# Nine pairs behind six plain units in the first projection, and a new order around its last pair

## The reference, cut to what matters

```python
def short_conv_fourier_mixer(h, w_in, conv_w, w_out):
    proj = h @ w_in                                  # 1024 -> 3072
    a_x, a_b, a_c, a_z, b_u, b_z = jnp.split(proj, ...)   # six parts of 512
    y_a = a_b * centred_depthwise_conv(a_c * a_x, conv_w) * jax.nn.silu(a_z)
    u = b_u.reshape(bsz, s, B_GROUPS, B_GROUP_DIM)
    f = jnp.fft.fft2(u, axes=(1, 3), norm="ortho").real
    y_b = f.reshape(bsz, s, B_WIDTH) * jax.nn.silu(b_z)
    return jnp.concatenate([y_a, y_b], axis=-1) @ w_out
x = x + short_conv_fourier_mixer(rms_norm(x, norm_even[i]), ...)
```

## Time and profile before

| What | us |
|---|---|
| median of three runs | 1758.22 |
| the profiled execution | 1759.79 |
| its span, first to last instruction | 1757.9 |
| PE busy | 1693.6 (96%) |
| VectorE (DVE) busy | 1158.4 (66%) |
| ScalarE (ACT) busy | 684.8 (39%) |
| GpSimd (POOL) busy | 486.8 (28%) |
| mean granted TensorE clock | 0.987 |
| PE's share of the chain that ended last | 83% |
| a load of w_raw, issue to landing | 4.1 |

### The profile page before, as it was taken

How to read it: one execution, slowest core, us unless ns; L and a number is a source line. 1 busy time by engine, 2 the same in 40 slices (tenths; PEclk the granted TensorE clock), 3 DMA queues, 4 the chain that set the end, 5 groups by cost and what they waited for, 6 DMA issues and landing times.

```text
span 1757.9 us, 21497 instructions
## 1 busy us (share of the span) xinstructions
PE 1693.6 (96%) x8228; PEld 1399.7 (80%) x8228; DVE 1158.4 (66%) x1421; ACT 684.8 (39%) x878; POOL 486.8 (28%) x348
## 2 busy tenths in 40 slices
PE   7699999899999999999899999999999999999997
PEld 6488887788788888888788877788888788878885
DVE  7867887445677777777876698345645267788323
ACT  7121112225566555666632422101123667772002
POOL 4244554233201111101013323223324322214330
PEclk9799999899999999999999999999999999999998
DMA  5011116132101111011242211112123311336102
GB/s 224 1 72 49 72 72 226 50 120 85 48 1 37 36 37 34 3 37 37 104 167 96 84 48 40 45 66 72 68 80 131 125 49 61 120 131 240 48 25 96
DMA packets 41829, 137.92 MB, mean 78 GB/s; under 512 B 5644, under 2 KB 6028, under 8 KB 41472
## 3 DMA queue, kind: packets, MB, share of 16 engines
q1 hardware_dynamic: 41440, 136.02, 21.5%
q10 hardware_dynamic: 288, 0.52, 0.1%
HBM read 104.81 MB, written 31.59 MB: 78 GB/s over the span
## 4 chain that ended last, share of the span: by engine, by line
PE 83%; DVE 11%; ACT 3%; issue 2%; DMA 0%; DVEq 0%; SPq 0%; ACTq 0%
PE pair L977 34%; PE pair L1164 11%; PE pair L1239 8%; PE pair L1302 5%; PE aux L1275 4%; PE pair L1288 3%; PE pair L988 2%; PE pair L1583 2%; PE aux L1454 1%; PE pair L996 1%; PE pair L1052 1%; PE aux L977 1%; PE pair L1568 1%; DVE stat_b L2558 1%; PE pair L1596 1%
## 5 line engine op out<-in xcount | busy, mean ns | idle before, releaser
L842 POOL CAST w_hi<-w_raw 128x1024 fp32r<-128x1024 f32 x86 | 96.4, 1121 | 942.0 <-issue 937.0
L844 POOL TENSOR_TENSOR w_lo<-w_raw,w_hi 128x1024 fp32r<-128x1024 f32 x86 | 217.3, 2527 | 6.9
L977 PE MATMUL pair<-op_hi,w_hi 128*128 128x512 f32 x670 | 207.4, 391 | 1.0 <-DVE op_lo L2202 0.7
L977 PE MATMUL pair<-op_lo,w_hi 128*128 128x512 f32 x670 | 206.9, 390 | 0.0
L977 PE MATMUL pair<-op_hi,w_lo 128*128 128x512 f32 x670 | 206.8, 390 | 0.0
L977 PEld LDWEIGHTS pair<-op_hi,w_hi 128*128 128x128 f32 x670 | 125.7, 188 | 30.0 <-issue 3.0
L977 PEld LDWEIGHTS pair<-op_hi,w_lo 128*128 128x128 f32 x670 | 126.0, 188 | 26.5
L977 PEld LDWEIGHTS pair<-op_lo,w_hi 128*128 128x128 f32 x670 | 126.1, 188 | 26.4
L1897 ACT ACTIVATE pt_hi<-pair 128x1024 fp32r<-128x1024 f32 x60 | 61.6, 1027 | 126.9 <-issue 84.7
L2197 DVE TENSOR_TENSOR pt_lo<-pair,pt_hi 128x1024 fp32r<-128x1024 f32 x60 | 73.5, 1224 | 52.7 <-ACT pt_hi L1897 48.9
L1239 PE MATMUL pair<-opb_hi,w_hi 128*128 128x512 f32 x256 | 101.8, 397 | 1.1 <-DVEq L136 0.6
(11 more groups left out here) (463 smaller groups left out, 3806.8 us busy)
## 6 DMA issues: line engine op xcount, KB each, us to landing
w_raw<-weight_units SPq DMA_DIRECT2D x106, 512.0 KB, 4.1
xa<-x_t SPq DMA_DIRECT2D x15, 512.0 KB, 7.7
xf<-y_dram SPq DMA_DIRECT2D x12, 512.0 KB, 4.6
x_dram<-xa SPq DMA_DIRECT2D x8, 512.0 KB, 5.8
xc<-x_dram SPq DMA_DIRECT2D x8, 512.0 KB, 7.8
x_dram<-xc SPq DMA_DIRECT2D x8, 512.0 KB, 2.7
y_dram<-y_d SPq DMA_DIRECT2D x8, 512.0 KB, 2.7
mz_dram<-y_d SPq DMA_DIRECT2D x8, 512.0 KB, 2.9
```

Of the source, the lines that this page charges most:

```text
L842: pool.tensor_copy(w_hi[:, u % 2, :], w_raw[:, u % RAW, :]).then_inc(w_hi_done, 1)
L844: pool.tensor_tensor(w_lo[:, u % 2, :], w_raw[:, u % RAW, :], w_hi[:, u % 2, :], ALU.subtract).then_inc(w_split, 1)
L977: mm = pe.matmul(acc[:, cols], w, x[:, kx, cols], start=(first and k == 0 and n == 0), stop=(last and k == KT - 1 and n == 2))
```

## The change

FAST becomes 6, so units 0 to 5 are plain and make the whole of group 0, and nine pairs follow. mixer_of, copy_at, the skipped slot in ring and GpSimd's wait behind it are renumbered to that. PE makes both transforms of group 0 among the plain units: over channels behind unit 4, over time behind unit 5. VectorE's queue ahead of the pairs holds folding, convolution, scalings and both outputs of group 0, with the operand sums and the first weight sums between them. In the last pair ScalarE makes high parts 0 and 1 of the second projection's operand between the copies of P5 and P6; VectorE makes the last group's fourier_output and low parts 0 and 1 between add_c11 and add_c22, and low parts 2 and 3 between add_c22 and add_c12.

```diff
--- before.py
+++ after.py
@@ -56,7 +56,7 @@
 UNITS = BASE[-1]
 
 
-FAST = 4
+FAST = 6
 PAIRS = (EVEN_IN - FAST) // 2
 QUAD = KT // 2
 RING_STEP = 8
@@ -90,13 +90,13 @@
 
 def copy_at(q, name):
 
-    order = ("P1", "P6", "P5") if q % 3 == 1 else ("P1", "P5", "P6")
+    order = ("P1", "P6", "P5") if q % 3 == 0 else ("P1", "P5", "P6")
     return COPIES + 3 * q + order.index(name) + 1
 
 
 def ring(at):
 
-    return (at + (2 if at >= RING_STEP else 0)) % 4
+    return (at + (1 if at >= RING_STEP else 0)) % 4
 
 
 def plain(n):
@@ -533,7 +533,7 @@
 
         def mixer_of(q):
 
-            return (q + 2) // 3, (q + 2) % 3
+            return q // 3 + 1, q % 3
 
         def updates(d):
 
@@ -889,7 +889,7 @@
                 if at < 4:
                     pool.wait_ge(unit_done, FAST - 1 + half)
                 else:
-                    pool.wait_ge(product_done, at - 1 if at - RING_STEP in (0, 1) else at - 3)
+                    pool.wait_ge(product_done, at - 2 if at - RING_STEP in (0, 1, 2) else at - 3)
                 pool.tensor_copy(hi, src).then_inc(w_hi_done, 1)
                 if name not in SUM_OF:
                     pool.wait_ge(w_hi_done, FAST + at + 1)
@@ -1168,15 +1168,16 @@
 
             for u in range(2, FAST):
                 unit(u, u, op_hi, op_lo, "even")
+                if u == FAST - 2:
+                    fft_channels(0)
+            fft_time(0)
             for q in range(PAIRS):
                 j, turn_of = mixer_of(q)
                 product(q, "P1")
                 if q >= 1:
                     product(q - 1, "P4")
                 product(q, "P5")
-                if q == 1:
-                    fft_time(0)
-                elif q >= 3 and turn_of == 2:
+                if turn_of == 2:
                     fft_time(j)
                 product(q, "P6")
                 product(q, "P2")
@@ -1184,8 +1185,6 @@
                     fft_channels(j)
                 product(q, "P7")
                 product(q, "P3")
-                if q == 0:
-                    fft_channels(0)
             product(PAIRS - 1, "P4")
             first_pair(BASE[1], "y1", op_hi, op_lo)
             for e in range(2, KT):
@@ -1738,7 +1737,7 @@
                 if kind == 0:
                     act.wait_ge(parts_ready, j)
                 elif kind == 1:
-                    act.wait_ge(c22_added, q - 1)
+                    act.wait_ge(c22_added, max(q - 1, 1))
                 else:
                     act.wait_ge(parts_ready, j + 1)
                 product_copy(q, "P1", first_row[kind][:, 0:HALF])
@@ -1779,26 +1778,28 @@
                 act.wait_ge(scaled_a, j + 1)
                 link(act.activation(y_a[:, 1, :], y_a[:, 1, :], ACT.Silu), silu_a)
 
-            copy_p1(0)
-            copy_p5(0)
-            copy_u2(0)
+            spectrum(0)
             fourier_gate(0)
-            spectrum(0)
-            for q in range(1, PAIRS):
+            conv_gate(0)
+            for q in range(PAIRS):
                 j, kind = mixer_of(q)
                 copy_p1(q)
                 if kind == 0:
-                    conv_gate(j - 1)
+                    if j >= 2:
+                        conv_gate(j - 1)
                     copy_u2(q)
                     copy_p5(q)
                     continue
                 if kind == 2:
                     fourier_gate(j)
                 copy_p5(q)
+                if q == PAIRS - 1:
+                    for k in range(2):
+                        y_hi("y1", k, y1_in[k], op_hi)
                 copy_u2(q)
                 if kind == 1:
                     spectrum(j)
-            for k in range(THROUGH["y1"]):
+            for k in range(2, THROUGH["y1"]):
                 y_hi("y1", k, y1_in[k], op_hi)
             conv_gate(AB - 1)
             for k in range(THROUGH["y1"], KT):
@@ -2383,29 +2384,38 @@
 
             dve.wait_ge(ax_ready, 1)
             by_token(ax_sb[:, :], ax_sb[:, :])
-            for n in range(3):
-                weight_sum(0, n)
             wait_job(dve, 2)
             link(dve.tensor_tensor(u_pad[:, 1:S + 1], pair[0][:, :], ax_sb[:, :], ALU.mult))
             free(2)
+            dve.wait_ge(bu_ready, 1)
+            fold_parts(0)
+            convolve(0)
             dve.wait_ge(copied, QUAD + 3)
             link(dve.tensor_tensor(xa_cmb[:, 0:QUAD, right], xa[:, 0:QUAD, right], xa_cmb[:, 0:QUAD, left], ALU.subtract),
                  cmb_low)
+            wait_job(dve, 4)
+            link(dve.tensor_tensor(cv[:, :], pair[0][:, :], cv[:, :], ALU.mult))
+            free(4)
+            for n in range(3):
+                weight_sum(0, n)
+            dve.wait_ge(ax_ready, 2)
+            by_token(sz_b[:, :], sz_b[:, :])
+            signal(scaled_b)
             dve.wait_ge(copied, QUAD + 2)
             link(dve.tensor_tensor(cmb_lo[:, 1], cmb_raw[:, 1], cmb_hi[:, 1], ALU.subtract), cmb_low)
             sum_low_part(0, "P5")
+            wait_job(dve, 5)
+            by_token(y_a[:, 1, :], pair[1][:, :])
+            signal(scaled_a)
+            free(5)
             sum_low_part(0, "P6")
             weight_sum(0, 3)
-            convolve(0)
+            fourier_output(0)
+            conv_output(0)
+            sum_low_part(0, "P7")
             dve.wait_ge(copied, QUAD + 4)
             link(dve.tensor_tensor(xa_cmb[:, QUAD:KT, left], xa[:, QUAD:KT, left], xa_cmb[:, QUAD:KT, right], ALU.subtract),
                  cmb_low)
-            sum_low_part(0, "P7")
-            dve.wait_ge(bu_ready, 1)
-            fold_parts(0)
-            dve.wait_ge(ax_ready, 2)
-            by_token(sz_b[:, :], sz_b[:, :])
-            signal(scaled_b)
             for q in range(PAIRS):
                 j, kind = mixer_of(q)
                 sum_low_part(q, "P3")
@@ -2413,9 +2423,16 @@
                 if q + 1 < PAIRS:
                     weight_sum(q + 1, 0)
                     weight_sum(q + 1, 1)
+                else:
+                    fourier_output(j)
+                    for k in range(2):
+                        low(k, y1_in[k], OP0["y1"])
                 add_c22(q)
                 if q + 1 < PAIRS:
                     sum_low_part(q + 1, "P5")
+                else:
+                    for k in range(2, QUAD):
+                        low(k, y1_in[k], OP0["y1"])
                 add_c12(q)
                 if q + 1 < PAIRS:
                     sum_low_part(q + 1, "P6")
@@ -2424,26 +2441,19 @@
                 if kind == 0:
                     fold_parts(j)
                     take_c21(q)
-                    if q + 1 < PAIRS:
-                        sum_low_part(q + 1, "P7")
+                    sum_low_part(q + 1, "P7")
                 elif kind == 1:
                     link(dve.tensor_tensor(u_pad[:, 1:S + 1], u_pad[:, 1:S + 1], ax_sb[:, :], ALU.mult))
                     convolve(j)
                     take_c21(q)
-                    if q + 1 < PAIRS:
-                        sum_low_part(q + 1, "P7")
+                    sum_low_part(q + 1, "P7")
                     signal(scaled_b)
                 else:
                     link(dve.tensor_tensor(cv[:, :], ab_row, cv[:, :], ALU.mult))
-                    if j == AB - 1:
-                        fourier_output(j)
-                        for k in range(QUAD):
-                            low(k, y1_in[k], OP0["y1"])
                     take_c21(q)
-                    if q + 1 < PAIRS:
-                        sum_low_part(q + 1, "P7")
                     signal(scaled_a)
                     if j < AB - 1:
+                        sum_low_part(q + 1, "P7")
                         fourier_output(j)
                     else:
                         for k in range(QUAD, THROUGH["y1"]):
```

## The result

The changed kernel takes 1741.75 us (median of four, 1741.51 to 1743.92) where the kernel before takes 1758.83 beside it: the ratio is 0.9905, 95% interval 0.9887 to 0.9922, so 17.1 us less. I forecast 1734 with a range of 1729 to 1741. The direction was right, and the gain is 70% of the 24.6 us forecast; the time lies 0.75 us above the range.

The account below looks back on a forecast made before the run. PE's time line bounds the kernel, its losses coming from VectorE's queue. Front -19.2 and end -5.4 give -24.6 from 1759.8, so 1735.2; less 1.6 for the median, 1734 us, range 1729 to 1741.

Parts of the forecast that it names:

- So 0.75 us of waiting, bounds 0 and 2.7: Group 1's transform: P6(1)'s later cast moves VectorE's queue 2.6 us, 1.8 to spare, so PE waits 0.75 us.
- the front: From first plain units to P4's end: waits and half-speed products ahead of the pairs go, P4 ends at 280.1, -19.2 us.
- the end: Behind the last pair: new ScalarE and VectorE order cuts losses from 12.0 to 6.6, -5.4 us, bounds 1 to 9.
- (a): Clock falls at the end, around high parts 6 and 7: 2.4 to 4 us more, 1737 us; chance 0.25.
- Against: 2.52 us did not, and each of my waits is below 2.1: Argument against (a): 2.52 us of idling left the clock up, and each forecast end wait is shorter than 2.1 us.
- (b): In front of P1(0): the 0.3 us to spare is missing, VectorE 2 to 4 us late, 1736 to 1740 us; chance 0.13.
- (c): GpSimd and VectorE collide less at end and front: -5.4 becomes -9, front waits go, 1729 us; chance 0.13.
- (d): VectorE's queue ahead of P1(0), stretched by GpSimd, becomes the bound: P1(0) 26 us late, 1762 us; chance 0.03.
- (e): The end gives nothing back, or a wait opens in each of three periods: 1739 to 1742 us; chance 0.03.
- Behind the stretch: After the unit following the first pair, starting near 308.4: no change; over 1 us difference would mean something missed downstream.

Follow-up runs that it names:

- shift4: Changed kernel plus four matmuls, overwritten by the next start, ahead of the second projection's fifth unit: 1744.29 us.
- front_only: Changed kernel with the old order around the last pair restored, keeping six plain units, nine pairs and the new front: 1745.2 us, ratio 0.9921.
- late_splits: Changed kernel with GpSimd's block splits of P1(2) and P4(1) allowed only one product later, ring unchanged: 1738.27 us, ratio 0.9882.
- end_only: Kernel before with only the new order around the last pair (four plain units, ten pairs): 1755.6 us, ratio 0.9978.
- ring4: Changed kernel with the weight ring's skipped slot moved from product 8 to product 4: 1738.53 us, ratio 0.9878.
- new_end: Skipped slot at product 4 as well, P6's copy ahead of all high parts, VectorE's low parts 3 to 7 last: 1733.96 us, ratio 0.9856.

## Why the prediction was right or wrong

**Which step failed.** "So 0.75 us of waiting, bounds 0 and 2.7", under the front, for the transform of group 1. The mechanism was right: the skipped slot moves the cast of P6(1) by a product, VectorE's queue by 2.6 us, and the folding follows. By the traces the folding starts 2.4 us later against the transform than in a later group of the kernel before (7.9 us ahead of where PE could have started it, where it was 10.3). The size was wrong in two ways. I took the folding's length from a later group, 8.6 us, where only one split stands beside most of it. But a queue that is later meets other work: here the next two splits, which made it 10.8 us. With 8.6 us the wait would have been the 0.75 us forecast. And I priced the wait as idle time only; 2.94 us of idling also brought the half speed, in four traces of four with this wait (both of the changed kernel, shift4, front_only), and with it 1.95 us more. Together 4.9 us instead of 0.75, 4.1 us of the 6.3 missing in the traces. The 1.8 us that this folding had to spare before (1.7 by PE's timeline, where the transform starts at 264.96) was a thin cover, and I applied the shared port at the end and in front, but not there.

**The rest of the front was right.** This execution was 1.1 us ahead already where GpSimd splits unit 4 (45.95 against 47.02), 0.6 of it in the first wait for weights (7.7 against 8.3 us). Unit 4 started at 57.07, where 58.2 less 1.1 gives 57.1; P1(0) did not wait, with y_a ready at 85.33 and PE there at 85.86, 0.5 to spare where I had 0.3. None of P5(0) to P4(0) waited. The front moved P6 of the last pair by 15.7 us; 19.2 - 4.1 + 1.1 = 16.2 was to be expected after the fact; 0.5 is unexplained.

**The end was right, wait by wait.**

| PE behind the last pair's P6 | forecast | changed kernel |
|---|---|---|
| P7 for ScalarE's copy | 2.0 | 1.94 |
| first pair for the bank | 1.8 | 1.38 |
| high part 6 | 1.1 | 0.70 |
| high part 7 | 1.7 | 1.56 |
| gain of the end | 5.4 | 5.4 |

The gain is 21.1 - 15.7. The waits are each a little shorter than forecast and the gain is not larger, because the profile counts idle time from the modelled end of the matmul before, and a restart costs a little too: in sum the stretch lost 6.7 us (42.1 less 156 x 0.227), where I had 6.6. That the gain agrees to 0.1 us is luck in part: in the second trace of before the stretch from P6 takes 46.96 us instead of 47.48, which makes it 4.9; and in shift4, where the clock fell at high part 7, the same code takes 43.7 us instead of 42.1. The exclusive lock on the ports that VectorE and GpSimd share (the Trainium skill, SBUF — State Buffer, section on the two separate sides of SBUF) was what made these numbers, and this trace agrees with it: low parts 2 and 3 together took 4.58 us in place of 2.5 beside GpSimd's splits, and c22 and c12, with an input in PSUM, took 0.69 us. VectorE's timeline there:

```profile
281.75 4.58 DVE L2198 TENSOR_TENSOR op_lo<-spec,op_hi 128x1024 fp32r<-128x1024 f32 x2
286.36 0.69 DVE L2374 TENSOR_TENSOR fold<-pair,fold 128x512 f32<-128x512 f32 x1
```

The same rule, applied at the folding, is the 2.7 us between late_splits and the changed kernel.

**Rivals.** (a) did not happen in the two traces of the changed kernel: the clock held through all four waits of the end, and in end_only and late_splits too. It can happen there, though, at about the chance given: in two of the six traces that have these waits the clock fell, in ring4 behind the 1.95 us in front of P7, for 1.3 us, and in shift4 behind the 1.56 us for high part 7, for 1.6 us. The price of 2.4 to 4 us was too high. Half speed was missed at the transform and again behind the stretch. "Against: 2.52 us did not, and each of my waits is below 2.1" read one row as a rule: other traces have the clock down after the same 2.5 us. (b), (c), (d) and (e) did not happen. The time is within (e)'s 1739 to 1742, but not by its reason: it put a wait in each of three periods, and there is one, in the first.

**Behind the stretch** I had costed 0 and named it as a sign of something missed. It is 2.8 us: 1.45 at the attention wait and 1.35 behind 1476 us, of which the second trace of before loses 0.9. That difference of some 2 us between executions belonged in the range.

The sum over the traces: 24.6 - 4.1 (transform) + 1.1 - 0.5 (start, unexplained) - 2.8 (behind) = 18.3.

## What to carry to other kernels

Where a step is moved later in a queue, take its length again at its new place: what runs beside it there is other work than where the row was read. A cover of under 2 us in a steady period is the first place to look when anything is pushed by one product. Price a wait of 1.5 us or more on PE as the wait and, with a chance, some 1.3 to 2 us of half speed behind it; here the clock fell behind 1 of 6 waits of 1.56 us, 1 of 6 of 1.95, 6 of 10 of 2.5 and 4 of 4 of 2.94. And put first in a queue what the next engine's last input waits for, not what is ready first: on ScalarE and VectorE together that was worth about 3 us here.

## What the runs showed of the hardware that was not expected

The same wait at the same place of the program ended at 2.4 GHz in some traces and at 1.2 GHz in others. The wait of 1.94 to 1.96 us in front of the last pair's P7: held in five, fell in one (ring4). The wait of 1.55 or 1.56 us for high part 7: held in five, fell in one (shift4). The wait of 2.50 to 2.52 us in the attention stage: held in four, fell in six. Those of 2.94 us at the transform fell in four of four, though in front_only the matmuls ran at full speed for a microsecond before the clock went down. Behind these waits the full speed was back 3 to 5 us after PE had resumed; behind the 7 us wait of the kernel before it took 7.5 to 9 us. No wait of 1.4 us or less at the end of the pairs was followed by it.

PE's timeline in new_end at the attention wait, where the clock held; the matmul behind it takes 0.39 us, and 0.58 in the changed kernel's row above:

```profile
809.04 0.39 PE L1301 MATMUL pair<-pt_hi,v_all 128*128 128x256 f32 x1 [2.51 <-DVE pt_lo L2195]
```
